# Attention pipeline with scores three steps ahead, and a fused bias-and-extreme instruction per head, in a one-core hybrid attention and mixture-of-experts block

## The reference

```python
def masked_softmax(logits, mask):
    return jax.nn.softmax(jnp.where(mask, logits, NEG_INF), axis=-1)
...
        s1 = jnp.einsum('bqhd,bkhd->bhqk', qb[:, :, :, 0], k1).astype(jnp.float32) * scale + bias
        s2 = jnp.einsum('bqhd,bkhd->bhqk', qb[:, :, :, 1], k2).astype(jnp.float32) * scale + bias
        a = masked_softmax(s1, mask) - lam * masked_softmax(s2, mask)
...
        s = (jnp.einsum('bqhd,bkhd->bhqk', qb, k).astype(jnp.float32) * scale
             + cq[..., :, None] - c[..., None, :])
...
        o = (gb[:, :, 0, :, :, None] * o_c + gb[:, :, 1, :, :, None] * o_s
             + gb[:, :, 2, :, :, None] * o_w)
```

## Time and profile before

| | |
|---|---|
| median of 3 runs | 2183.83 us (2181.47 to 2188.8) |
| the profiled execution | 2185.85 us, span of its instructions 2184.0 us |
| TensorE busy | 1835.5 us (84% of the span) |
| VectorE busy | 638.7 us (29%) |
| ScalarE busy | 477.5 us (22%) |
| GpSimd busy | 461.3 us (21%) |
| attention | about 147 to 880 us from the span's start |
| experts' stream of weights | about 1075 to 2120 us, 400 GB/s |

### The profile page before, as it was taken

How to read it: one execution, slowest core, us unless ns; L and a number is a source line. 1 busy time by engine, 2 the same in 40 slices (tenths; PEclk the granted TensorE clock), 3 DMA queues, 4 the chain that set the end, 5 groups by cost and what they waited for, 6 DMA issues and landing times. The chain is left out here.

```text
span 2184.0 us, 27742 instructions
## 1 busy us (share of the span) xinstructions
PE 1835.5 (84%) x11130; PEld 1284.6 (59%) x11130; DVE 638.7 (29%) x1270; ACT 477.5 (22%) x1005; POOL 461.3 (21%) x340
## 2 busy tenths in 40 slices
PE   6999999999999977999748878888788888787870
PEld 4887777776666654888635545554455555454530
DVE  4433334436665577100321111111111111111115
ACT  4222323323434343222201010101010101010101
POOL 2333323332221120344121111111111111111100
PEclk9999999999999987999969999999999999999995
DMA  9552222332131120233539999999999999999966
GB/s 266 125 160 77 77 59 78 77 74 52 39 68 49 44 111 1 68 99 95 234 146 421 420 423 421 422 420 423 421 422 421 420 421 422 420 421 418 416 252 249
DMA packets 206614, 527.21 MB, mean 241 GB/s; under 512 B 65922, under 2 KB 149154, under 8 KB 162122
## 3 DMA queue, kind: packets, MB, share of 16 engines
q1 hardware_dynamic: 187738, 509.15, 61.2%
q0 software_dynamic: 18800, 17.00, 2.3%
HBM read 530.38 MB, written 46.03 MB: 264 GB/s over the span
## 5 line engine op out<-in xcount | busy, mean ns | idle before, releaser
L790 PE MATMUL PJ<-ht_rounded,ring_rounded 128*128 128x512 f32 (+1 forms) x928 | 322.7, 401 | 4.5 <-ACT at_region L1148 3.8
L1031 PE MATMUL PJ<-ht_region,ring_region 128*64 128x256 f32 x1024 | 254.7, 412 | 65.7 <-DMA ht_region<-in_w_up 65.7
L1031 PE MATMUL PJ<-at_region,ring_region 128*64 128x256 f32 x1024 | 243.2, 399 | 58.5 <-DMA at_region<-in_w_up 57.6
L1032 PE MATMUL PJ<-ht_region,ring_region 128*64 128x256 f32 x1024 | 255.4, 413 | 0.0
L1032 PE MATMUL PJ<-at_region,ring_region 128*64 128x256 f32 x1024 | 243.9, 399 | 0.0
L1031 PEld LDWEIGHTS PJ<-ht_region,ring_region 128*64 128x64 f32 x1024 | 150.2, 149 | 152.9 <-issue 96.5
L728 POOL DMA_INDIRECT y_scratch<-ring_region,s_idx x64 | 64.6, 1009 | 789.8 <-DVE ring_region L1653 765.2
L1031 PEld LDWEIGHTS PJ<-at_region,ring_region 128*64 128x64 f32 x1024 | 145.1, 144 | 139.9 <-issue 90.0
L676 POOL TENSOR_TENSOR ring_rounded<-ring_region,at_rounded 128x2048 fp32r<-128x2048 f32 (+1 forms) x31 | 139.7, 4505 | 346.3 <-ACT at_rounded L1093 346.3
L676 POOL TENSOR_TENSOR ring_rounded<-ring_region,ring_rounded 128x2048 fp32r<-128x2048 f32 x30 | 137.7, 4591 | 322.6 <-ACT ring_rounded L1093 322.6
L1645 DVE TENSOR_TENSOR ring_region<-ring_region,PJ 64x256 f32<-64x256 f32 x64 | 27.1, 423 | 603.6 <-ACT ring_region L1294 603.6
(11 more groups left out here) (242 smaller groups left out, 2632.7 us busy)
## 6 DMA issues: line engine op xcount, KB each, us to landing
at_region<-in_w_gate SPq DMA_DIRECT2D x32, 2048.0 KB
at_region<-in_w_up SPq DMA_DIRECT2D x32, 2048.0 KB
at_region<-in_w_down SPq DMA_DIRECT2D x32, 2048.0 KB, 22.6
ht_region<-in_w_gate SPq DMA_DIRECT2D x32, 2048.0 KB
ht_region<-in_w_up SPq DMA_DIRECT2D x32, 2048.0 KB
x_region<-in_w_down SPq DMA_DIRECT2D x32, 2048.0 KB
ring_region<-in_w_in SPq DMA_DIRECT2D x36, 1024.0 KB, 5.9
ring_region<-in_w_out SPq DMA_DIRECT2D x16, 1024.0 KB, 5.2
```

Of the source, the lines that this page charges most:

```text
L790: ins = mm(out, w[:, k, 0:width], h[:, k, :], start=k == 0 and i == 0, stop=k == KT - 1 and i == 2)
L1031: mm(GU[0:CAP, 0:D_EXPERT], x, gate[:, j, :], start=j == 0, stop=j == KT - 1)
L1032: ins = mm(GU[CAP:2 * CAP, 0:D_EXPERT], x, up[:, j, :], start=j == 0, stop=j == KT - 1)
```

## The change

It does four things. (1) `LOOK` becomes 3: TensorE's order is now `fill(n, 0)`, `values(n - 1)`, `transpose_probs(n)`, `fill(n, 1)`, `scores(n + 3)`; ACT's is `after_fill(n, 0)`, `out_copy(n - 1)`, `copy_pT(n)`, `exps(n + 2)`, `after_fill(n, 1)`; DVE's is `after_fill(n, 0)`, `row_max(n + 2)`, `normalise(n + 1)`, `copy_pT(n)`, `after_fill(n, 1)`. All buffers stay as they are. (2) In diff and nsa steps the scores are computed with a minus sign (Q and the bias strip are scaled by -1 where they are copied anyway), and `row_max` becomes: a minimum over the far columns of both heads, where there are any (W over 256), then for each head one `tensor_tensor_reduce` that adds the bias to the near columns and takes the minimum, beginning from the far one. `exps` gets scale -1. Fox steps are computed as before. (3) The product of inverse sum and gate (or -lambda) is no instruction of its own any more: `tensor_scalar` gets both factors. (4) `fillings()` puts the three projections of unit 1 into the two slots of step 0.

```diff
-LOOK = 2
-
+LOOK = 3
+
+SIGN = {"diff": -1.0, "fox": 1.0, "nsa": -1.0, "cmp": -1.0, "slc": -1.0, "win": -1.0}
...
         slots = [(n, half) for n in range(lo, hi) for half in range(2)]
-        slots = slots[:-1] if len(slots) > 4 else slots
+        if len(slots) < 4:
+            (n, half), last = slots[0], slots[-1]
+            for i in range(FIRST[g + 1], FIRST[g + 2]):
+                out[n][half].append((i, 0, KT, False))
+                n, half = last
+                if COLUMNS[i][1] == "v":
+                    out[n][half].append((i, KT, KT, True))
+            continue
+        slots = slots[:-1]
...
             for n in range(ALL_STEPS):
                 fill(n, 0)
+                if n >= 1:
+                    values(n - 1)
                 transpose_probs(n)
+                fill(n, 1)
                 if n + LOOK < ALL_STEPS:
                     scores(n + LOOK)
-                fill(n, 1)
-                values(n)
+            values(ALL_STEPS - 1)
...
-                    ins = fn(q_live[g % 2][name == "q1"], unit0.get(n, PJ[:]), ACT.Copy, scale=SCALE)
+                    ins = fn(q_live[g % 2][name == "q1"], unit0.get(n, PJ[:]), ACT.Copy, scale=SIGN[kind] * SCALE)
...
-            fn(strip_sb[0:T5_HEADS, :], Oflat[0:T5_HEADS, 0:STRIP], ACT.Copy).then_inc(strip_copied, 1)
+            fn(strip_sb[0:T5_HEADS, :], Oflat[0:T5_HEADS, 0:STRIP], ACT.Copy, scale=-1.0).then_inc(strip_copied, 1)
...
                         ins = fn(probs[:, par, half, 0:(qb + 1) * P], S[:, par, half, 0:(qb + 1) * P], ACT.Exp,
-                                 bias=nmx[:, par, half:half + 1], accum_out=rsum[:, par, half:half + 1])
+                                 bias=nmx[:, par, half:half + 1], scale=SIGN[kind], accum_out=rsum[:, par, half:half + 1])
...
             exps(0)
+            exps(1)
             for n in range(ALL_STEPS):
-                if n + 1 < ALL_STEPS:
-                    exps(n + 1)
+                after_fill(n, 0)
                 if n >= 1:
                     out_copy(n - 1)
-                after_fill(n, 0)
                 copy_pT(n)
+                if n + 2 < ALL_STEPS:
+                    exps(n + 2)
                 after_fill(n, 1)
...
-                else:
-                    near = min(W, 2 * P)
-                    sc = S[:, par, :, W - near:W]
-                    if kind == "diff":
-                        b = bias[0][:, u:u + 1, 2 * P - near:2 * P].broadcast_to([P, 2, near])
-                    else:
-                        b = bias[(u + 1) % 2][:, 2 * pr:2 * pr + 2, 2 * P - near:2 * P]
-                    link(v.tensor_tensor(sc, sc, b, ALU.add))
-                v.tensor_reduce(nmx[:, par, :], S[:, par, :, 0:W], AX_X, ALU.max, negate=True).then_inc(max_ready, 1)
+                    v.tensor_reduce(nmx[:, par, :], S[:, par, :, 0:W], AX_X, ALU.max, negate=True).then_inc(max_ready, 1)
+                    return
+                near = min(W, 2 * P)
+                if near < W:
+                    link(v.tensor_reduce(far_min[:, par, :], S[:, par, :, 0:W - near], AX_X, ALU.min))
+                for half in range(2):
+                    sc = S[:, par, half, W - near:W]
+                    b = bias[0][:, u, 2 * P - near:2 * P] if kind == "diff" else \
+                        bias[(u + 1) % 2][:, 2 * pr + half, 2 * P - near:2 * P]
+                    ins = v.tensor_tensor_reduce(sc, sc, b, 1.0, far_min[:, par, half:half + 1] if near < W else -NEG,
+                                                 ALU.add, ALU.min, nmx[:, par, half:half + 1])
+                ins.then_inc(max_ready, 1)
...
                     link(v.reciprocal(rinv[:, par, :], rsum[:, par, :]))
-                    link(v.tensor_tensor(coef[:, par, 0:1], neglam, rinv[:, par, 1:2], ALU.mult))
-                    link(v.tensor_scalar(p2, p2, coef[:, par, 0:1], None, ALU.mult))
+                    link(v.tensor_scalar(p2, p2, rinv[:, par, 1:2], neglam, ALU.mult, ALU.mult))
...
-                    if kind != "fox":
-                        which = NSA_HEADS * (1 if kind == "slc" else 2) + u * 4 + pr * 2
-                        link(v.tensor_tensor(coef[:, par, :], gates[:, qb, which:which + 2], c, ALU.mult))
-                        c = coef[:, par, :]
-                    v.tensor_scalar(p1, p1, c[:, 0:1], None, ALU.mult)
-                    ins = v.tensor_scalar(p2, p2, c[:, 1:2], None, ALU.mult)
+                    which = NSA_HEADS * (1 if kind == "slc" else 2) + u * 4 + pr * 2
+                    for half, p in enumerate((p1, p2)):
+                        if kind == "fox":
+                            ins = v.tensor_scalar(p, p, c[:, half:half + 1], None, ALU.mult)
+                        else:
+                            ins = v.tensor_scalar(p, p, c[:, half:half + 1], gates[:, qb, which + half:which + half + 1],
+                                                  ALU.mult, ALU.mult)
...
-            for n in range(LOOK):
-                row_max(n)
+            row_max(0)
+            row_max(1)
             normalise(0)
             for n in range(ALL_STEPS):
                 after_fill(n, 0)
-                copy_pT(n)
+                if n + 2 < ALL_STEPS:
+                    row_max(n + 2)
                 if n + 1 < ALL_STEPS:
                     normalise(n + 1)
-                if n + LOOK < ALL_STEPS:
-                    row_max(n + LOOK)
+                copy_pT(n)
                 after_fill(n, 1)
```

More of the change, by code:

```diff
@@ L378, in hybrid_block_moe_kernel @@
         nmx = tiny(2, 2)
+        far_min = tiny(2, 2)
         cmx = tiny(2, 2)
@@ L382, in hybrid_block_moe_kernel @@
         csum = tiny(2, 2)
-        coef = tiny(2, 2)
         ccoef = tiny(2, 2)
@@ L1200, in exps @@
                     ins = fn(probs[:, par, 0, 0:P].rearrange("p (h n) -> p h n", h=2), S[:, par, :, 0:2 * CMP_PAD],
-                             ACT.Exp)
+                             ACT.Exp, scale=-1.0)
                 else:
@@ L1445, in row_max @@
                     sc = S[:, par, :, 0:2 * CMP_PAD].rearrange("p h (u n) -> p h u n", u=2)
-                    link(v.tensor_tensor(sc, sc, bcast(bcast(cmask[:, qb, :], 1, 2), 1, 2), ALU.add))
-                    link(v.tensor_reduce(cmx, sc, AX_X, ALU.max))
+                    link(v.tensor_tensor(sc, sc, bcast(bcast(cmask[:, qb, :], 1, 2), 1, 2), ALU.subtract))
+                    link(v.tensor_reduce(cmx, sc, AX_X, ALU.min))
                     v.tensor_tensor(sc, sc, bcast(cmx, 3, CMP_PAD), ALU.subtract).then_inc(max_ready, 1)
```

## The result

The changed kernel takes 2194.76 us in the median (2191.66 to 2196.24, 6 runs), the kernel before beside it 2184.49 us. The ratio is 1.0045, 95% interval 1.0032 to 1.0058: slower by more than the 0.3% that a measurement can tell. The profiled execution took 2191.66 us, its span is 2189.5 us (before 2184.0).

The account below looks back on a forecast made before the run. TensorE was taken to bound the attention's fills, and a scaling, row-maximum, exponentials loop through VectorE and ScalarE the last unit. 19 (last unit) + 19 + 4 (fills) - 4 (start) = 38 us less gave 2146 us, range 2130 to 2173.

Parts of the forecast that it names:

- D: Rival: slower than before, the fused instruction far below one element a step, from 1.65 us each; at 2.0 us, 2206; chance 0.06.
- The fused instruction: VectorE's row extreme: each fused add-and-minimum over 256 elements taken at 0.44 us, between 0.34 and 0.88.
- Scaling by two factors: VectorE's scalings: a second factor leaves their time unchanged, 1.0 us a step at W = 512 without the coefficient product.
- B: Rival: fused instruction dear at 0.88 us each and scaling rate halved, 13 to 16 us lost, 2160; chance 0.13.
- A late ACT copy is covered by some 3 us or more of matmuls ... I take 19 as gone: Stretch with fills: values behind fill(n, 0) no longer wait for ScalarE's copy; 19 of 20.6 + 3.5 us saved.
- the stalls go to the next scaling: Last unit: two GpSimd stalls, 6.2 us in all, move from the removed product to the next scaling; no gain booked.
- under 4 us: Argument against the rival that only the last unit gains: a GpSimd stall of VectorE lasts under 4 us.
- The 9.0 us for turned V tiles stay: Stretch with fills: TensorE's 9.0 us of waits for ScalarE to take turned V tiles out of PJ stay unchanged.
- With fewer waits half comes back: 4: Stretch with fills, 516 to 792 us: of about 8 us lost to TensorE's low clock, 4 us come back.
- The last unit: Part without fills: the loop through ScalarE opens, reciprocals of steps 93 to 111 span 49 to 57 us; 19 us less.
- The start: Attention's start: third scores wait 2.8 us uncovered, plus about 1 us for a copy out of PJ; 4 us lost.
- Rival A: Only the last unit gains; 24 us of fill waits come back elsewhere; 15 us less, 2169; chance 0.14.

Follow-up runs that it names:

- e3: The kernel before, in its old order (LOOK 2), with only the fused row extreme and the scaling by two factors: 2174.18 us, 0.9965.
- e1: The changed kernel with VectorE copying PT ahead of the next scaling instead of behind it: 2187.18 us, 1.0014 of the kernel before.
- e9: The changed kernel with ScalarE rounding later weights behind its other copies, and lone turned V tiles copied ahead of the exponentials: 2188.98 us, 1.0015 of the kernel before.
- e5: The changed kernel with ScalarE's exponentials moved behind after_fill(n, 1): 2198.16 us, 1.0059 of the kernel before.
- e2: The changed kernel's order (LOOK 3) with the row maximum, coefficient product and signs of the kernel before: 2199.96 us, 1.0078 of the kernel before.
- e10: The changed kernel with PT copied ahead of the scaling, GpSimd's split in four, third scores behind the first fill, and late rounding: 2158.29 us, 0.9871.
- e12: The kernel before with fused instructions, two-factor scaling, GpSimd's split in four, and ScalarE's rounding at the end of a round: 2156.8 us, 0.9868.
- e16: The kernel before with fused instructions, two-factor scaling, GpSimd's split in four, values behind the first fill, and rounding at the round's end: 2150.01 us, 0.9836.
- e4: The changed kernel with each GpSimd weight split as four instructions instead of one: 2182.82 us, 0.9992 of the kernel before.

## Why the prediction was wrong

The forecast was 2146 us, the result 2195; it lies outside the range, and the 0.06 for "slower" was for another mechanism (D).

**The fused instruction: right.** Taken at 0.44 us, it occupies VectorE 0.41 us from start to next start with its result read (802.63 to 803.04 to 803.44). Scaling by two factors kept its rate: 1.00 us for two of 128x512, as in the earlier trace rows. e3 measured this half at 8 us. B and D were about its price and are out.

**"A late ACT copy is covered by some 3 us or more of matmuls ... I take 19 as gone": the failed step.** Those waits went, but I asked only what comes ahead of `values` on TensorE, not what now stands ahead of its operand on VectorE. The order puts `copy_pT(n)` behind `normalise(n+1)`, which the stalls of the earlier trace rows hit. I had written that the stalls go to the next scaling, and priced them in the last unit; I never followed them into the fills, where one falls on the end of each of four nsa projections. Measured: 17.8 us of new waits up to 792 us and 7.24 at 809.61, ahead of the step from which my last part counts; e1 shows their releaser. The cover was mis-sized as well: in the nsa units a piece of fill ahead of `values` lasts 1.6 us at most, at three of the four places it is 1.0 us, and at the fourth there is none. And a stall isn't "under 4 us": the scaling at 803.65 was held for 4.80.

**"The 9.0 us for turned V tiles stay": wrong.** They were 7.6 (the doubled wait above) and became 17.4. Turn and next projection follow each other as before, but ScalarE's queue between them grew. e9 brings them to 7.9 by moving the rounding and the exponentials; with the exponentials moved alone (e5) they don't shrink.

**"With fewer waits half comes back: 4" of the clock: wrong sign.** Behind waits of 5 to 7 us the clock was low where behind 1.4 us ones it had not been. From 147 to 792 us the windows give (183 x 0.03 + 186 x 0.01 + 276 x 0.04) / 0.5 = 37 us at the low level, for 16.6 by the earlier trace rows. The price is read from the stretch with fills: the same 3292 matmuls kept TensorE busy 6.2 us longer.

**The last unit: right, its size too.** VectorE's idle time before the reciprocals for ScalarE fell from 10.4 to 1.3 us, the loop through ScalarE is open, and the reciprocals of steps 93 to 111 span 53.9 us (823.69 to 877.56; forecast 49 to 57, before 72.9). From step 89 on the gain is 21.2 us, or 20 without the scores of step 91, for 19; the clock there is 0.86 for 0.73 (forecast 0.9). What was wrong is its division: I let VectorE bound a step and so made the fused instruction part of the gain, but e2, without it, takes the same 73.4 us, and e3, with it and the old order, 85.5. Once the loop is open, the 0.55 us a step of W = 512 that it was to save on VectorE (1.96 to 1.61 and 1.2 to 1.0) are worth nothing there.

**The start: right.** A 2.54 us wait of the third scores (forecast 2.8), 3.5 us in all for 4.

In sum: 38 forecast = 19 + 19 + 4 - 4; measured -4.5 = 21.2 - 22.2 - 3.5 at the output projection. Rival A had the shape: the last unit gains in full, and the waits of the fills come back elsewhere, with ScalarE in front of the turned tile as it said. But it let about as much come back as had gone, for a sum of 15 us less; here TensorE's idle time in the fills went from 31.0 to 47.0 us. The deeper order isn't slow in itself: with the repairs of e10 it beats the kernel before by 28 us. But the same (e12) comes with `LOOK = 2`, the fused instruction, quarters and late rounding. Whether the deeper order is worth anything once all waits are mended stays open; e16 is 8 us ahead of e10, and the two differ in more than the depth.

## What to carry to other kernels

When an order is rewritten, look up for every engine what now stands behind the instruction that another engine can stall, and whether its waiter has cover at each place, the ends of units above all. Work that nobody needs soon (here the rounding of weights two tiles ahead, 1.9 us) belongs behind the copies that free a buffer: moving it won 11 us in the kernel before by itself. And a wait "for ACT" is a question about ACT's queue, not yet an answer: read what it did just before.

## What the runs showed of the hardware

One GpSimd instruction of 4.49 us (803.68 to 808.17) held a scaling of some 0.5 us for 4.80 us, from 803.65 to 808.45; the scaling behind it was quick. Cut in four, each of two scalings takes 1.48 us and ends 0.3 us behind one piece of the split (588.07 + 1.28 and 588.15 + 1.48, then 589.30 + 1.45 and 589.55 + 1.48 in e10): VectorE gets in once between two pieces. The Trainium skill ("SBUF — State Buffer", Summary: rules for kernel authors) says that when VectorE is in a 2-port mode beside GpSimd, the second of the two to issue blocks fully until the first has finished. The trace agrees with the full block: the scaling ended 0.28 us behind the split. Which of the two issued first can't be read from starts of 803.65 and 803.68.

Behind the wait of 6.35 us at 608.7 the next 5 us had a granted clock of 0.57, and behind the other three waits of 5 us and more it was low as well (0.50 to 0.66 in 507 to 512, 707 to 712 and 810 to 815 us). Waits of 1.42 us left 1.00. In between, the length of the wait does not settle it. A wait of 2.54 us ahead of the third scores was followed by 0.55 in the changed kernel (149 to 154 us), and the same wait in e4 and e9 by 1.00 (152 to 157, 151 to 156). A wait of 2.94 us left 1.00 in the changed kernel (464 to 469 us) and 0.62 in e1 (465 to 470). So clock losses read from single traces, as in the sums above, are uncertain by that much.

The fused instruction leaves its result by a second one of 0.14 us, which begins before the profile's end of the first (0.41 us after a start with a duration of 0.49), so durations of such pairs must not be added; starts tell their price.
